# Mixture of experts: token rows through DRAM by indexed copies, last expert peeled, weights split in halves

## The reference, cut to what matters

```
logits = (h @ router_w).astype(float32)
top_v, top_i = lax.top_k(logits, 2)
top_w = softmax(top_v)
gates = einsum('btk,btke->bte', top_w, one_hot(top_i, 8))
out = 0
for e in range(8):
    out = out + gates[..., e:e + 1] * ((silu(h @ w_gate[e]) * (h @ w_up[e])) @ w_down[e])
x = x + gate_mod * rms_norm(out)
```

## Time and profile before

| | |
|---|---|
| runs, median (lowest to highest) | 1841.51 us (1840.03 to 1843.41) |
| the profiled execution, its time | 1841.8 us |
| its span, first to last instruction | 1840.0 us |
| mean granted TensorE clock | 0.959 of full |
| PE busy, share of the span | 1739.8 us, 95% |
| PE weight loads, DVE, ACT busy | 76%, 59%, 51% |
| POOL busy | 7.6 us |
| read from HBM, written | 401.10 MB, 1.05 MB |
| loads of 1 MB, median time to landing | 4.8 us |

### The profile page before, as it was taken

One profiled execution on the slowest core, in us unless ns is written; L12 is line 12 of the kernel. 1 busy time (PEld: TensorE's weight loads), 2 busy tenths in 40 slices (PEclk: granted clock), 3 DMA queues, 4 the chain that ended last, 5 costly groups with the idle time before them and its releaser, 6 DMA issues.

```text
span 1840.0 us, 23247 instructions
## 1 busy us (share of the span) xinstructions
PE 1739.8 (95%) x8946; PEld 1392.2 (76%) x8946; DVE 1083.2 (59%) x1140; ACT 935.7 (51%) x1109; POOL 7.6 (0%) x10
## 2 busy tenths in 40 slices
PE   6998999899999999799888999999999999999996
PEld 3685459688888788479677788888888888888884
DVE  2441231433223233453554898988888889898896
ACT  3512432532222232442464677767677777777774
POOL 0000000000000000000001000000000000000000
PEclk8998999889999999989996999999999999999998
DMA  8424473543222222122125798989898989899880
GB/s 313 166 90 183 148 258 122 194 176 129 98 92 92 92 92 97 55 92 92 46 83 196 300 376 318 374 325 368 324 368 338 351 343 349 348 346 372 321 313 24
DMA packets 59682, 403.10 MB, mean 219 GB/s; under 512 B 7904, under 2 KB 10720, under 8 KB 11104
## 3 DMA queue, kind: packets, MB, share of 16 engines
q1 hardware_dynamic: 59616, 402.17, 58.1%
HBM read 401.10 MB, written 1.05 MB: 219 GB/s over the span
## 4 chain that ended last, share of the span: by engine, by line
PE 85%; DVE 6%; ACT 4%; issue 2%; DMA 2%; DVEq 0%; SPq 0%; ACTq 0%
PE ps L1463 23%; PE ps L1465 23%; PE ps L1464 23%; PE ps L1481 2%; PE ps L1505 2%; DMA raw<-in_w 2%; PE ps L1834 2%; PE ps L1619 1%; PE ps L1514 1%; PE ps L1866 1%; ACT wh L861 1%; DVE x L1391 1%; PE ps L1668 1%; PE ps L1650 1%; ACT raw L505 1%
## 5 line engine op out<-in xcount | busy, mean ns | idle before, releaser
L1367 DVE TENSOR_TENSOR wl<-raw,wh 128x2048 fp32r<-128x2048 f32 x266 | 609.0, 2292 | 98.0 <-ACT wh L861 97.7
L861 ACT ACTIVATE wh<-raw 128x2048 fp32r<-128x2048 f32 x266 | 509.8, 1916 | 148.5 <-PE ps L1465 148.5
L1463 PE MATMUL ps<-ah,wh 128*128 128x512 f32 (+1 forms) x848 | 304.5, 359 | 16.6 <-DVE al L965 9.2
L1463 PE MATMUL ps<-wh,ah 128*128 128x512 f32 (+1 forms) x808 | 314.2, 389 | 0.0
L1465 PE MATMUL ps<-wh,al 128*128 128x512 f32 (+1 forms) x808 | 306.1, 379 | 0.0
L1464 PE MATMUL ps<-wl,ah 128*128 128x512 f32 (+1 forms) x808 | 305.1, 378 | 0.0
L1464 PE MATMUL ps<-al,wh 128*128 128x512 f32 (+1 forms) x848 | 296.1, 349 | 0.0
L1465 PE MATMUL ps<-ah,wl 128*128 128x512 f32 (+1 forms) x848 | 296.1, 349 | 0.0
L935 DVE TENSOR_TENSOR wl<-raw,wh 128x1024 fp32r<-128x1024 f32 x120 | 141.5, 1222 | 103.1 <-ACT wh L462 103.1
L1463 PEld LDWEIGHTS ps<-ah,wh 128*128 128x128 f32 x848 | 163.8, 193 | 44.8 <-issue 10.1
L1464 PEld LDWEIGHTS ps<-al,wh 128*128 128x128 f32 x848 | 164.2, 194 | 20.7 <-issue 1.2
(11 more groups left out here) (238 smaller groups left out, 1755.2 us busy)
## 6 DMA issues: line engine op xcount, KB each, us to landing
raw<-in_w SPq DMA_DIRECT2D x377, 1024.0 KB, 4.8
x<-in_x SPq DMA_DIRECT2D x1, 2048.0 KB, 11.5
raw<-in_ukv SPq DMA_DIRECT2D x1, 1024.0 KB, 5.6
out<-x SPq DMA_DIRECT2D x8, 128.0 KB, 1.9
raw<-in_uq SPq DMA_DIRECT2D x3, 256.0 KB, 3.9
raw<-in_dft SPq DMA_DIRECT2D x1, 512.0 KB, 4.4
raw<-in_uq SPq DMA_DIRECT2D x3, 128.0 KB, 4.2
cst<-in_cst SPq DMA_DIRECT2D x1, 320.0 KB, 11.8
```

What stands on the lines that cost most here:

```text
L861: act.activation(wh[:, J % SPLITS, :], slot(J % SLOTS), ACT.Copy).then_inc(w_hi, 1)
L1367: dve.tensor_tensor(wl[:, J % SPLITS, :], slot(J % SLOTS), wh[:, J % SPLITS, :].bitcast(F32), ALU.subtract).then_inc(w_lo, 1)
L1463: pe.matmul(out, lh, rh, start=start, stop=False)
```

## The change

Two DRAM tensors are added, `sent` and `back`, each with 256 rows of 1024 values for each expert. POOL issues all copies to and from them.

- `zeros` (POOL, once PE has begun the dense layer) is copied over both tensors, 32 copies of 512 KB. ACT and DVE wait for them before they take y2.
- The token rows `tok` are made by one DVE instruction each for a half row of a token half, in float32, without rounding. POOL no longer adds or clears anything.
- DVE works out for each token two row numbers (its two experts, with its ranks in them) and two gates. Four indirect copies send the token rows to `sent`. SP loads slot 9 now last, after these have landed.
- `gather` is eight float32 transpositions of an expert's rows, which POOL has fetched from `sent` into `came`. ACT rounds them and DVE subtracts from PSUM. On ACT this stands now ahead of the split of entry 27 and ahead of hidden group 9; on DVE it stands behind both.
- An expert's result is copied from PSUM by one ACT instruction, unscaled, and POOL copies it to `back`. `select`, `selT`, `scatter` and the additions to `acc` are gone.
- The loop runs seven times. The eighth expert has a body of its own without the gather and without group 0 of a next expert (31 pieces); group 10 is turned behind ("d", 8).
- At the end, indirect copies bring for each token its two result rows back, DVE weighs and adds them, ACT makes the norm row by row, PE turns the rows, and one DVE instruction a chunk adds them to the stream.
- Each piece of the experts' weights is rounded and subtracted in two halves of 1024 values.

The diff, cut to its core:

```diff
+LAST_ORDER = [o for o in ORDER if o[0] == "d" or o[1]]
+LAST_TURN = {q: g for q, g in TURN.items() if q <= GATHER}
+LAST_TURN[GATHER + 1] = 10
...
+        tok = area(12288, 2, D)
+        zeros = area(11264, D)
+        came, y = (x[:, a:a + 4, TL:T] for a in (0, 4))
...
@@ SP @@
-            still_used = (EARLY_SLOTS, SLOTS - 1)
+            still_used = (EARLY_SLOTS, SLOTS - 1, SLOTS - 2)
+                if j == SLOTS - 2:
+                    sp.wait_ge(sem("first_ps"), 2)
+                    sp.wait_ge(sem("rows_moved"), 16 * SENT)
...
@@ ACT @@
-            for t, h in tok_parts[0:2]:
-                tokens(t, h)
...
-                    act.activation(wh[:, J % SPLITS, :], slot(J % SLOTS), ACT.Copy).then_inc(w_hi, 1)
+                    for h in range(2):
+                        act.activation(wh[:, J % SPLITS, piece_half(h)], slot(J % SLOTS)[:, piece_half(h)], ACT.Copy).then_inc(w_hi, 1)
...
+                def result(e, pieces, banks):
+                    act.wait_ge(w_used, PER_EXPERT * e + at.used + 2 + pieces)
+                    act.wait_ge(sem("rows_moved"), 16 * e + 16 * (SENT + at.done))
+                    act.activation(y[:, 0:2 * banks, :], ps[:, 3:3 + banks, :].rearrange("p b (t n) -> p (b t) n", t=2), ACT.Copy
+                                   ).then_inc(sem("y_ready"), 1)
+                def body(e, order, turn):
+                    hidden_hi(e, 0)
+                    for q, (kind, g, half) in enumerate(order):
+                        if kind == "gu" and half == 1:
+                            silu(g, PER_EXPERT * e + (at.used + 2 + q + 1))
+                        if q == GATHER and order is ORDER:
+                            gathered(e + (at.done + 1))
+                        if order is ORDER or q + 2 + AHEAD < 2 + len(LAST_ORDER):
+                            split_next(e, 2 + q + AHEAD)
+                        if turn.get(q):
+                            hidden_hi(e, turn[q])
+                    result(e, len(order), 2 if order is ORDER else 1)
...
+                with act.Fori(0, NE - 1) as e:
+                    body(e, ORDER, TURN)
+                body(NE - 1, LAST_ORDER, LAST_TURN)
...
+            for t in range(2):
+                act.wait_ge(sem("y_sum"), t + 1)
+                act.activation(spare_row[:, t, :], last_row[:, t, :], ACT.Square, accum_out=out_ss[:, t:t + 1]).then_inc(sem("y_ss"), 1)
...
+                act.activation(last_row[:, t, :], last_row[:, t, :], ACT.Copy, scale=out_rinv[:, t:t + 1]).then_inc(sem("y_ss"), 1)
...
@@ DVE @@
+            for t, h in tok_parts:
+                dve.scalar_tensor_tensor(out=tok[:, t, 512 * h:512 * h + 512], in0=ps[:, 2 * t + h, :], scalar=tok_rinv[:, t:t + 1],
+                                         in1=shiftB[:, 2 * h:2 * h + 2, :].rearrange("p a b -> p (a b)"), op0=ALU.mult, op1=ALU.add
+                                         ).then_inc(sem("tok_f32"), 1)
...
+                    for h in range(2):
+                        dve.wait_ge(w_hi, 2 * PER_EXPERT * e + (2 * (MAIN + J) + h + 1))
+                        ins = dve.tensor_tensor(wl[:, J % SPLITS, piece_half(h)], slot(J % SLOTS)[:, piece_half(h)],
+                                                wh[:, J % SPLITS, piece_half(h)].bitcast(F32), ALU.subtract)
+                    ins.then_inc(w_lo, 1)
...
+                        if kind == "gu" and half == 1:
+                            hidden(g, 11 * e + (at.hid + (g or 11) + 1))
+                        if q == GATHER + 1 and order is ORDER:
+                            gathered(e + (at.done + 1))
+                        if order is ORDER or q + 2 + AHEAD < 2 + len(LAST_ORDER):
+                            split_next(e, 2 + q + AHEAD)
+                        if turn.get(q):
+                            hidden_lo(e, turn[q])
...
+                dve.tensor_copy(y[:, 2:4, :], ps[:, 4, :].rearrange("p (t n) -> p t n", t=2)).then_inc(sem("y_rest"), 1)
...
@@ POOL @@
+            for n in range(2 * NE):
+                pool.dma_start(sent[n * P:(n + 1) * P, :], zeros).then_inc(sem("rows_cleared"), 16)
+                pool.dma_start(back[n * P:(n + 1) * P, :], zeros).then_inc(sem("rows_cleared"), 16)
...
+            for c in range(SENT):
+                pool.indirect_dma_start(sent[:, :], rows(c), tok[:, c % 2, :], None).then_inc(sem("rows_moved"), 16)
+            pool.wait_ge(sem("rows_moved"), 16 * SENT)
...
+                fetch(1, at.done if no else None)
+                with pool.Fori(0, NE - 2) as e:
+                    keep(e)
+                    fetch(e + 2, e + (at.done + 1))
+                keep(NE - 2)
...
+                for t in range(2):
+                    pool.indirect_dma_start(first_row[:, t, :], None, back[:, :], rows(t)).then_inc(sem("first_rows"), 16)
+                pool.wait_ge(sem("first_rows"), 16 * 2 * (no + 1))
+                pool.wait_ge(sem("y_rest"), no + 1)
+                keep(NE - 1)
...
+            for t in range(2):
+                pool.indirect_dma_start(last_row[:, t, :], None, back[:, :], rows(2 + t)).then_inc(sem(f"last_rows{t}"), 16)
...
@@ PE @@
+            def gather(count):
+                pe.wait_ge(sem("came"), 16 * count)
+                for k in range(KD):
+                    mm = pe.transpose(ps[:, 6 + k // 4, (k % 4) * P:(k % 4 + 1) * P], came[:, k // 2, (k % 2) * P:(k % 2 + 1) * P], ident)
+                mm.then_inc(sem("xe_ps"), 1)
...
+                        if q == GATHER and order is ORDER:
+                            gather(e + (at.done + 1))
+                        if q in turn:
+                            g = turn[q]
+                            if q >= GATHER:
+                                pe.wait_ge(sem("hT_lo"), 11 * e + (at.turned + (g or 11)))
+                            turn_hidden(g, 11 * e + (at.hid + (g or 11) + 1))
```

More of the change, by code:

```diff
@@ L338, in build @@
         cond_ready, modv_ready, scales_ready = map(sem, ("cond_ready", "modv_ready", "scales_ready"))
-        USED = 2 + NE * PER_EXPERT
-        GROUPS = 11 * NE
+        SENT = 4
         class Pass:
             def __init__(self, no):
[L348 to L355, removed]
+                self.J = PIECES * no
+                self.used = MAIN + PIECES * no
+                self.hid = 11 * NE * no
+                self.turned = 11 * NE * no
+                self.done = NE * no
         early_landings = [len(RING) // EARLY_SLOTS] * EARLY_SLOTS + [0] * (SLOTS - EARLY_SLOTS)
@@ L366, in half @@
             return slice(h * (PIECE // 2), (h + 1) * (PIECE // 2))
+        piece_half = half
         def slot(n):
@@ L709, in _ @@
             act.wait_ge(sem("hid_lo"), NF)
+            act.wait_ge(sem("rows_cleared"), 16 * 4 * NE)
             for q in range(2):
@@ L793, in first_split @@
                 act.wait_ge(w_used, MAIN - SPLITS + j + 1)
-                act.activation(wh[:, j, :], slot(j), ACT.Copy).then_inc(w_hi, 1)
+                for h in range(2):
+                    act.activation(wh[:, j, half(h)], slot(j)[:, half(h)], ACT.Copy).then_inc(w_hi, 1)
             for p in range(4):
@@ L882, in experts @@
                         split_next(0, j)
-                    gathered(at.gathered + 1)
+                    gathered(at.done)
                 else:
@@ L1412, in experts @@
                 split_next(0, AHEAD + 1)
[L1413 to L1432 removed]
+                with dve.Fori(0, NE - 1) as e:
+                    body(e, ORDER, TURN)
+                body(NE - 1, LAST_ORDER, LAST_TURN)
+                dve.wait_ge(w_used, at.used + PIECES)
+                dve.wait_ge(sem("rows_moved"), 16 * (SENT + at.done + NE - 1))
+                dve.tensor_copy(y[:, 2:4, :], ps[:, 4, :].rearrange("p (t n) -> p t n", t=2)).then_inc(sem("y_rest"), 1)
             experts(0)
@@ new lines, in _ @@
+            experts(0)
+            pool.wait_ge(sem("count_ready"), 1)
+            most = pool.value_load(cnt[0:1, 0:1], min_val=0, max_val=TL)
+            with pool.If(most > P):
+                pool.wait_ge(sem("rows_moved"), 16 * (SENT + NE))
+                experts(1)
+                pool.wait_ge(sem("rows_moved"), 16 * (SENT + 2 * NE))
+            pool.wait_ge(sem("rows_moved"), 16 * (SENT + NE))
+            for t in range(2):
+                pool.indirect_dma_start(last_row[:, t, :], None, back[:, :], rows(2 + t)).then_inc(sem(f"last_rows{t}"), 16)
@@ L1926, in _ @@
                 experts(1)
-            sum_squares(N_OF)
+            for t in range(2):
+                pe.wait_ge(sem("y_ss"), 2 * t + 2)
+                for k in range(KD):
+                    mm = pe.transpose(ps[:, k // 2, (k % 2) * TL + t * P:(k % 2) * TL + (t + 1) * P], last_row[:, t, k * P:(k + 1) * P], ident)
+                    if t and k % 2:
+                        mm.then_inc(sem("y_turned"), 1)
 def mla_units():
```

339 lines of the change are left out of this document (137 added, 202 removed).

## The result

The changed kernel takes **1796.09 us** (median; 1794.99 to 1798.73) against 1840.77 (1839.92 to 1843.41) of the kernel before on the same chip: 0.9757 of it, interval 0.974 to 0.9774. That is 44.7 us saved, 34.7 were forecast; 1796 lies in the lower part of the range (1780 to 1822), beside rival B (1799). The profiled execution has a span of 1794.5 (1840.0 before), so 45.5 are to be found in the trace.

A forecast was written before the change was run, and what follows sets the result against it. PE was taken to bound the expert loop, with DVE and ACT close behind. Loop 16.8, last expert 11.0, front 2.5 and tail 4.4 sum to 34.7 off 1841.8, giving 1807 us; range 1780 to 1822.

The forecast's parts named there:

- rival B: Expert loop: the stall at group 9 is there but the clock does not fall; 1799 us, chance 0.16.
- Scatter, selection, gates out: Experts 0 to 6: removing these saves 3.18 us each; the ACT copy in their place is covered.
- Rival A: Expert loop: no stall at group 9, a period at 94; 1782 us, chance 0.14.
- The clock: Expert loop: five of seven new stalls followed by half clock, costing 1.2 us an expert, bounds 0 and 1.7.
- The last expert 11.0: Peeled last expert: 12.4 us of work goes, a wait before group 10's transposition loses 1.4; 11.0 saved.
- Halves, 0.8, at the front alone: Weight pieces in halves are ready sooner; pays once, before the first transposition: 0.8 us.
- Step 3: Gather: PE stalls 2.1 us before group 9's down piece, DVE subtracting it behind the split; bounds 0 and 3.4.
- The front, 2.5: Before the first transposition: POOL's additions gone, gather slightly shorter, halves; 2.5 us earlier, bounds 0 and 5.
- POOL's copies cost nothing: Clearing, indirect and per-expert copies fit within DMA: 35.7 MB an expert at 367 GB/s against 383; no cost, only just.
- Rival C: Expert loop: DMA is the bound, an expert taking 99.0 us at 360 GB/s; 1820 us, chance 0.10.
- Rival E: Expert loop: POOL's copies come late and PE waits for gathered rows, 7 us an expert; 1856 us, chance 0.05.
- The tail 23.4: Last transposition to end: 23.4 us with two DRAM steps, against 27.85 before; 4.4 saved, bounds 18 and 30.

The follow-up runs named there:

- experiment 1: Changed kernel with ACT and DVE handling hidden group 9 first, then the gathered rows, then the split: 1779.12 us, 0.9642 of the kernel before.
- experiment 7: Changed kernel with group 9 put first on ACT alone, DVE still making the split before subtracting group 9: 1801.91 us, one run.
- experiment 8: Changed kernel with four unused POOL additions of 128x512 put back beside DVE's ranking: 1804.97 us, one run.
- experiment 10: Kernel of experiment 1 with twelve more DRAM-to-DRAM copies of 512 KB in each of six loop turns: 1821.95 us, one run.
- experiment 2: Changed kernel with weight pieces rounded and subtracted whole instead of in halves: 1811.13 us, 0.9806 of the kernel before.
- experiment 4: Kernel before with only the last expert peeled (scatter and selection stay, second pass left out): 1832.95 us, 0.9934.
- experiment 6: Kernel of experiment 1 with six more DRAM-to-DRAM copies of 512 KB in each of six loop turns: 1782.05 us, one run.

## Why the prediction was right, and where it was not

The direction, the places and most sizes held. The forecast case as it was written had two parts, a stall and a clock that falls behind it; the second did not happen, and so the outcome is rival B's, to which 0.16 was given. The forecast's own bounds, 1796 to 1817, are narrower than its bounds for clock, tail and front added up (1791 to 1820), and the time lies on their lower edge.

1. *Scatter, selection, gates out:* right. The plain group takes 8.42, and nothing of them is left in the period (eleven groups 92.6, gather 0.87, stall 2.2).
2. *Gather 1.0:* 0.87.
3. *A stall of 2.1 at group 9, the subtraction behind a split:* right in place, engine and cause, 1.91 in all seven, and with the restart 2.2. Experiments 1 and 7 show that the order is the cause. Rival A (no stall, a period at 94) is what the kernel does once the order is mended.
4. **The clock: this step failed.** "I let five of seven be followed so: 1.2 us an expert". None of seven was: no stretch at half clock between 1003 and 1773 us. The price of a fall was well taken (1.6 measured, bound 1.7); its frequency was not. It came from one row for each side, 2.00 with a fall and 1.5 without. What the runs show in its place: after gaps of 1.91, none of seven here and one of seven in experiment 8; of 2.40, two of seven; of 2.70, three of seven; of 4.3 to 6.0, five of five in experiment 10. Equal gaps were followed by a fall or not, in one execution; these counts are too small for a rule. The row that the step rests on was no good sample of the loop: the gap of 2.00 at the first transposition was followed by a fall in all three traces that have it (before, experiments 2 and 4), the one of 1.97 or 1.98 in the last expert in neither of two (experiments 2 and 4). What decides between them stays open. Seven times 1.2, 8.4 of the 10.8 us by which the trace saved more than was forecast, are this step. One fall less is also in expert 0: in the kernel before it had come behind the gap at the first transposition, which is 1.22 now, and its turn took 100.36 for 99.46.
5. *The last expert 11.0:* 10.9, with a gap of 1.18 for the 1.4 forecast.
6. *Halves, 0.8, at the front alone:* the price of 0.8 for a wait is right, the place too narrow. It was worked out against the kernel before, whose loop in the changed form has a wait for a split in each turn and one in the last expert. Step 3 had the halves in its walk (3.44) and so in its sum; that whole pieces would have cost nine waits and the clock, 9 to 14 us in all (experiment 2), was not said.
7. *The front, 2.5:* 4.0. POOL's share of it is right: the earlier trace rows has 1.24 and 0.80 for what now takes 0.29 and 0.17. The stream reached this place 1.0 later in this execution, and the first gather began 0.65 earlier, so 1.7 for the 1.6 forecast. The term that was missed is the clock's: it rose at about 1002.9, within the gather, instead of 1008.8, behind it. So the gather took 5.2 for 6.9, and the first products behind it came 0.23 apart instead of 0.42, another 0.9. With the halves' 0.8 that is 4.0. The prediction had this in its bound of 5 and not in its sum. The stretch of the gather in the table by stage, before and after (the clock is the third number from the end), and the first transposition after:

```profile
1000.09:1006.97 6.88, 6.88 (x32) 6.88 (x33) 3.11 (x6) 3.84 (x4) 1.80 (x1) 0.50 0.91 375
...
999.44:1004.90 5.46, 5.46 (x33) 5.46 (x34) 2.91 (x18) 0.60 (x1) 2.96 (x3) 0.69 0.88 326
```

```profile
1011.58 0.44 PE L1904 MATMUL ps<-cst,sq 128*128 128x128 f32 x2 [1.22 <-DVE sq L1379]
```

8. *POOL's copies cost nothing:* right. The clearing copies raise the DMA share to 1.02 at 400 to 440 us, and PE is busy throughout:

```profile
400.00:420.00 20.00, 20.00 (x169) 20.00 (x168) 5.98 (x7) 4.94 (x7) 12.51 (x24) 1.00 1.02 368
420.00:440.00 20.00, 20.00 (x94) 16.70 (x93) 7.58 (x15) 4.78 (x6) 0.00 (x0) 1.00 1.02 415
```

"But only just" was wrong. The 383 GB/s, taken as the rate over the share, was no limit: the measured one is about 413, and six copies more, 3.1 MB an expert, cost nothing (experiment 6). Rival C is refuted by experiments 6 and 10 together. The Trainium skill, DMA: Bandwidth & Descriptors, "Where 436 GB/s comes from", has the HBM side bind at about 358 GB/s; this core alone sustained 373 to 414. Rival E did not come up: POOL's fetch is asked for a whole expert ahead, and lands 10.6 us after its issue with DVE busy nine tenths of the time.

9. *The tail 23.4:* 24.4. Its chain:

```profile
1772.00 0.78 POOL L1470 DMA_DIRECT2D back<-x  x1 [32.20 <-DVE x L1414]
...
1775.67 1.40 POOL L1497 DMA_INDIRECT raw<-back,ints  x1 [2.89 <-DMA back<-x]
...
1780.36 1.28 DVE L1429 SCALAR_TENSOR_TENSOR raw<-raw,small 128x1024 f32<-128x1024 f32 x1 [4.13 <-DMA raw<-back,ints]
...
1787.40 1.97 PE L1951 MATMUL ps<-cst,raw 128*128 128x128 f32 x8 [0.81 <-ACT raw L913]
1788.13 3.23 DVE L1433 SCALAR_TENSOR_TENSOR x<-ps,scl,x 128x256 f32<-128x256 f32 x8 [4.26 <-PE ps L1951]
```

The copy out takes 3.7 (1772.00 to 1775.67), the rows' way back 4.7: bounded from SP's rows at 4.4 each, and close. From the last product to the copy's issue it is 1.9 where 0.9 was taken; that is the term that was most short. The end behind the last DVE instruction took 3.1 for 2.5, and the eight DVE instructions 3.2 for 3.8.

## What to carry to other kernels

When an instruction is put ahead of others on one engine, walk the queues of all engines that wait for what now stands behind it. Here a rounding and a subtraction that stood behind a split on ACT and DVE, the same in all seven turns, were worth 17 us, and the test was to put them first. A price may be sure and its frequency not: of a clock that falls behind a wait, ask how large the wait is and on how many rows the rule rests, and keep both outcomes as cases. A DMA share near 1 does not say that DMA is the bound; look for waits on landings, and load it further to see where they begin.

## What was not expected of the hardware

- DMA's share reads 0.97 at 373 GB/s and 1.01 at 414: with more asked of them the engines move more at nearly the same share. The limit for this mix on one core lay at about 413 GB/s.
- Half-clock stretches behind equal gaps of PE came in some turns and not in others (0 or 1, 2, and 3 of 7 for 1.91, 2.40 and 2.70 us), and behind all five gaps of 4.3 to 6.0 us.
- Beside POOL's additions a DVE instruction on 128 x 2 values took 1.26 us instead of 0.17.
